# Three transformer blocks on one core: norms, values, state decays and gates of the second block's mixers at other places in the engines' orders

## The reference, cut to what matters

```python
qkv = jax.nn.silu(causal_short_conv(jnp.concatenate([a_q, a_k, a_v], -1), gdn_conv)).astype(f32)
aq = l2_normalize(to_chunks(aq, GDN_HEADS)) * (GDN_DK ** -0.5)
ak = l2_normalize(to_chunks(ak, GDN_HEADS))
o_a = from_chunks(gated_delta_rule(aq, ak, av, beta, scalar_to_chunks(g_a)))
...
o_b = from_chunks(diag_decay_linear_attention(bq, bk, bv, to_chunks(log_alpha, GLA_HEADS)))
...
o_c = from_chunks(diag_decay_linear_attention(cq, to_chunks(k_c, HGRN_HEADS), ...))
...
y = (jax.nn.sigmoid(m_a) * (o_a @ w_br_a) + jax.nn.sigmoid(m_b) * (o_b @ w_br_b)
     + jax.nn.sigmoid(m_c) * (o_c @ w_br_c))
return y @ w_out
```

## Time and profile before

| | |
|---|---|
| median of 3 runs | 4140.33 us |
| the profiled execution | 4149.57 us, of it span 4147.8 |
| TensorE busy in the span | 3614.0 us (87%) |
| VectorE, ScalarE, GpSimd busy | 1619.3, 1226.5, 170.5 us |
| mean granted clock of TensorE | 0.893 |
| the mixers of the second block | 1904.3 to 2775.2 us |
| the branches' start | 2775.2 to 2807 us |

### The profile page before, as it was taken

One profiled execution on the slowest core, in us unless ns is written; L12 is line 12 of the kernel. 1 busy time (PEld: TensorE's weight loads), 2 busy tenths in 40 slices (PEclk: granted clock), 3 DMA queues, 4 the chain that ended last, 5 costly groups with the idle time before them and its releaser, 6 DMA issues. The chain is left out here.

```text
span 4147.8 us, 67008 instructions
## 1 busy us (share of the span) xinstructions
PE 3614.0 (87%) x29006; PEld 2801.7 (68%) x29006; DVE 1619.3 (39%) x2889; ACT 1226.5 (30%) x2001; POOL 170.5 (4%) x129
## 2 busy tenths in 40 slices
PE   7888989888889989996877777769899999888998
PEld 6676767666669989994655556657678777445444
DVE  2443344434344353424434344546543343322121
ACT  2322232232222122223333445541222221233330
POOL 0000000000002010000101001120000000000000
PEclk9898889889769989997888889989899999978887
DMA  3000001000013323320111111123133333201110
GB/s 121 23 30 24 25 28 30 24 25 27 20 63 92 108 62 92 92 87 26 54 49 41 41 43 60 52 104 94 49 91 92 92 92 92 76 11 36 41 36 36
DMA packets 63590, 236.23 MB, mean 57 GB/s; under 512 B 7232, under 2 KB 7232, under 8 KB 62144
## 3 DMA queue, kind: packets, MB, share of 16 engines
q1 hardware_dynamic: 57168, 209.16, 16.7%
q0 software_dynamic: 2672, 16.50, 1.0%
q10 hardware_dynamic: 3456, 6.29, 0.4%
HBM read 219.28 MB, written 12.65 MB: 56 GB/s over the span
## 5 line engine op out<-in xcount | busy, mean ns | idle before, releaser
L405 PE MATMUL psum<-arena,ring 128*128 128x264 f32 (+2 forms) x5304 | 1625.0, 393 | 7.3 <-DVE arena L350 6.2
L405 PE MATMUL psum<-arena,arena 128*128 128x264 f32 (+1 forms) x6288 | 1538.5, 348 | 100.3 <-DVE ring L341 34.5
L405 PE MATMUL psum<-arena 32*32 32x32 f32 (+16 forms) x16392 | 1126.4, 248 | 364.3 <-ACT arena L326 112.5
L405 PEld LDWEIGHTS psum<-arena 32*32 32x32 f32 (+10 forms) x16392 | 790.4, 138 | 714.1 <-issue 317.2
L405 PEld LDWEIGHTS psum<-arena,arena 128*128 128x128 f32 x6288 | 1040.4, 194 | 277.8 <-issue 83.2
L405 PEld LDWEIGHTS psum<-arena,ring 128*128 128x128 f32 (+1 forms) x5304 | 966.3, 196 | 255.9 <-issue 127.3
L334 ACT ACTIVATE arena<-psum 128x512 f32<-128x512 f32 (+12 forms) x601 | 268.0, 446 | 1046.4 <-PE psum L405 905.1
L341 DVE TENSOR_TENSOR ring<-ring,arena 128x1024 fp32r<-128x1024 f32 (+1 forms) x301 | 362.3, 1204 | 475.3 <-ACT arena L334 470.7
L341 DVE TENSOR_TENSOR arena<-arena 128x528 f32<-128x528 f32 (+9 forms) x692 | 330.9, 478 | 411.0 <-ACT arena L326 262.1
L334 ACT ACTIVATE arena<-ring 128x1024 fp32r<-128x1024 f32 (+1 forms) x301 | 308.8, 1026 | 569.0 <-PE psum L405 513.7
L341 DVE TENSOR_TENSOR arena<-arena,psum 88x192 f32<-88x192 f32 (+4 forms) x428 | 193.4, 452 | 573.9 <-PE psum L405 566.0
(11 more groups left out here) (35 smaller groups left out, 680.1 us busy)
## 6 DMA issues: line engine op xcount, KB each, us to landing
ring<-in_w SPq DMA_DIRECT2D x368, 512.0 KB, 3.5
bg<-arena ACTq DMA_DIRECT2D x24, 256.0 KB, 2.0
ring<-in_w SPq DMA_DIRECT2D x24, 256.0 KB, 2.6
arena<-in_x SPq DMA_DIRECT2D x2, 2112.0 KB, 11.7
arena<-bg POOLq DMA_DIRECT2D x1, 3072.0 KB, 16.8
od<-arena POOLq DMA_DIRECT2D x8, 264.0 KB, 2.3
arena<-od POOLq DMA_DIRECT2D x1, 2112.0 KB, 8.8
out<-arena SPq DMA_DIRECT2D x1, 2048.0 KB, 6.3
```

The costliest lines, as they stand in the source:

```text
L405: self.last_ins = self.eng.matmul(out, l, r, start=start, stop=stop, skip_group_check=skip)
```

## The change

Six things:

1. `delta()`: the sum of squares of q is issued after k's projection, that of k after v's; ScalarE's and VectorE's parts are placed accordingly, with the copies and subtractions for the next weights ahead of silu and convolution.
2. `delta()`: `gd_kk`, `gd_kq` and the transposes of v and k come before `gd_row` and wait for the scaled keys (`gd_qk`) alone; the decay matrices are made behind them, the exp `gd_er` last.
3. `linear()`: the gate's projection stands before the transposes of the values; the gate's silu and the copy of the transposed values are both after them.
4. `decay_attention`: `la_last`, the exps and `la_qi` are part of the last level's step.
5. Gates: their banks are emptied by a copy. The sigmoids are taken in the branches, in place, one behind each slab's high copy.
6. O's split: both halves on VectorE, 11 of 12 pieces at the end of VectorE's `delta()`, one per step as they become ready, the twelfth at the start of the branches. GpSimd's 12 subtractions are gone.

The diff, cut to its core:

```diff
+    def values(off, r, i, gate):
         yield from glin(off, ("la_proj", r, "v", i), ("la_vt", r, i))
         yield
+        yield from glin(off + SLAB, ("la_proj", r, "g", i), gate)
         P.wait_ge(*at("la_vt", r, i))
         b = P.bank(1, "la_v", r, i)
...
-            for i, nme in enumerate("qkv"):
-                yield from glin(off + i * SLAB, ("gd_proj", hd, i), ("gd_pad", hd, i))
-                if hd == 0:
-                    (rates, sums, turned)[i]()
-                if nme != "v":
-                    yield
-                    P.colsum(("gd_sum", hd, i), ("gd_root", hd, i), c["ones"], [U.n0 if nme == "q" else U.u], T, [("gd_sq", hd, i)])
+            def squares(i):
+                P.colsum(("gd_sum", hd, i), ("gd_root", hd, i), c["ones"], [U.u if i else U.n0], T, [("gd_sq", hd, i)])
+
+            yield from glin(off, ("gd_proj", hd, 0), ("gd_pad", hd, 0))
+            if hd == 0:
+                rates()
+            yield
+            yield from glin(off + SLAB, ("gd_proj", hd, 1), ("gd_pad", hd, 1))
+            if hd == 0:
+                sums()
+            squares(0)
+            yield
+            yield from glin(off + 2 * SLAB, ("gd_proj", hd, 2), ("gd_pad", hd, 2))
+            if hd == 0:
+                turned()
+            squares(1)
+            yield
...
-            P.wait_ge(*at("gd_ct"))
-            b = P.bank(1, "gd_diff", hd)
-            for j in range(4):
-                P.mm(bk(b)[:, J4[j]], s16[0:16, 4 * j + hd, :], m.CT[0:16])
-            P.did("gd_row", hd)
-            yield
-
-            P.wait_ge(*at("gd_qi", hd))
+            P.wait_ge(*at("gd_qk", hd))
             four(("gd_kk", hd), ("gd_A", hd), U.k, U.k)
             four(("gd_kq", hd), ("gd_M", hd), U.k, U.q)
-            P.wait_ge(*at("gd_conv", hd, 2))
             P.wait_ge(*at("gd_silu", hd, 2))
...
+            yield
+            P.wait_ge(*at("gd_ct"))
+            b = P.bank(1, "gd_er", hd)
+            for j in range(4):
+                P.mm(bk(b)[:, J4[j]], s16[0:16, 4 * j + hd, :], m.CT[0:16])
+            P.did("gd_row", hd)
...
-            A.act(m.sg, bk("b_gate", i), ACT.Sigmoid, "b_gate", i)
+            A.copy(m.sg, bk("b_gate", i), "b_gate", i)
...
-                x = (U.q, U.k, U.v)[i]
                 A.act(x, x, ACT.Silu, "gd_silu", hd, i)
...
+                if i < 2:
+                    A.act(U.u if i else U.n0, x, ACT.Square, "gd_sq", hd, i)
+
+            def root(i):
+                A.wait_ge(*at("gd_sum", hd, i))
+                A.inv_root(U.wT if i else U.n1, bk("gd_root", hd, i), "gd_root", hd, i, bias=c["eps6"])
...
+            act_more(K, m.wx)
+            yield
+            silu(0)
...
+            act_more(K, m.wx)
+            yield
+            silu(1)
+            root(0)
...
+            act_more(K, m.wx)
+            yield
+            silu(2)
+            root(1)
...
-            A.wait_ge(*at("gd_row", hd))
-            A.act(U.er, bk("gd_diff", hd), ACT.Exp, "gd_er", hd)
+            yield
             A.wait_ge(*at("gd_diff", hd))
             A.act(U.DT, U.D, ACT.Relu, scale=-1.0)
             A.act(U.D, U.D, ACT.Relu)
-            A.act(U.D, U.D, ACT.Exp, scale=-1.0)
-            A.act(U.DT, U.DT, ACT.Exp, "gd_decay", hd, scale=-1.0)
-            yield
+            A.act(U.D, U.D, ACT.Exp, "gd_decay", hd, scale=-1.0)
+            A.act(U.DT, U.DT, ACT.Exp, "gd_decayt", hd, scale=-1.0)
+            A.act(U.er, bk("gd_er", hd), ACT.Exp, "gd_er", hd)
```

```diff
+            else:
+                cu = v4(W.cum)
+                A.wait_ge(*at("la_last", r))
+                A.act(W.E, W.E, ACT.Exp)
+                A.act(m.el[:, 0:4].unsqueeze(2), cu[:, :, 127:128], ACT.Exp)
+                A.act(W.cum, W.cum, ACT.Exp, "la_exps", r)
             yield GATES
         gate_out()
-        cu = v4(W.cum)
-        A.wait_ge(*at("la_last", r))
-        A.act(W.E, W.E, ACT.Exp)
-        A.act(m.el[:, 0:4].unsqueeze(2), cu[:, :, 127:128], ACT.Exp)
-        A.act(W.cum, W.cum, ACT.Exp, "la_exps", r)
...
+        act_more(K, m.wx)
+        yield
+        yield
         A.wait_ge(*at("la_vtr", r, i))
+        A.act(m.Gt[i], bk(*gate), ACT.Silu, *gate)
         A.copy(m.V[i], bk("la_v", r, i), "la_v", r, i)
...
+            dve_more(K, m.wx)
+            conv(0)
...
+            dve_more(K, m.wx)
+            conv(1)
...
+            V.wait_ge(*at("gd_root", hd, 0))
+            V.stt(U.q, U.q, 128.0 ** -0.5, U.n1, MUL, MUL)
+            yield
+            dve_more(K, m.wx)
...
+            V.wait_ge(*at("gd_root", hd, 1))
+            V.stt(U.k, U.k, 1.0, U.wT, MUL, MUL, "gd_qk", hd)
+            yield
...
+            V.wait_ge(*at("gd_row", hd))
+            V.tt(v4(U.D), v4(bk("gd_er", hd)), col("cu"), SUB, "gd_diff", hd)
+            V.wait_ge(*at("gd_decay", hd))
+            V.tt(v4(U.D), v4(U.D), bc4(c["slo"]), MUL)
+            for j, J in enumerate(J4):
+                V.stt(U.A[:, J], bk("gd_A", hd)[:, J], G["nbe"][:, 4 * j + hd:4 * j + hd + 1], U.D[:, J], MUL, MUL, *(("gd_A", hd) if j == 3 else ()))
+            V.wait_ge(*at("gd_decayt", hd))
+            V.tt(v4(U.DT), v4(U.DT), bc4(c["triu"]), MUL)
+            V.tt(U.M, bk("gd_M", hd), U.DT, MUL, "gd_M", hd)
+            V.wait_ge(*at("gd_er", hd))
+            V.tt(U.qi, U.q, U.er, MUL, "gd_qi", hd)
...
+            ready.add(hd)
+        for j in range(11):
+            while j not in ready:
+                yield
+            split_dve(V, m.Oh_r[j][:], m.O[:, j * T:j * T + T], m.O_r[j][:], "b_Osplit", j)
+            yield
...
+            else:
+                cu = v4(W.cum)
+                V.wait_ge(*at("la_K", r, n))
+                V.tt(v4(W.E), cu[:, :, 127:128].to_broadcast([128, 4, 128]), cu, SUB, "la_last", r)
+                V.wait_ge(*at("la_s", r, n - 1, heads - 1))
+                V.wait_ge(*at("la_exps", r))
+                V.tt(W.Kz, W.k, W.E, MUL)
+                V.tt(W.Q, W.q, W.cum, MUL, "la_qi", r)
...
-        cu = v4(W.cum)
-        V.wait_ge(*at("la_K", r, len(LV) - 1))
-        V.tt(v4(W.E), cu[:, :, 127:128].to_broadcast([128, 4, 128]), cu, SUB, "la_last", r)
-        V.wait_ge(*at("la_exps", r))
-        V.tt(W.Kz, W.k, W.E, MUL)
-        V.tt(W.Q, W.q, W.cum, MUL, "la_qi", r)
```

```diff
+GATE_PART = (0, 1, 2, 2, 3, 3, 3, 3)
...
-        pe_lin3(K, m.wb, i, ("b_y", i), m.Oh_r, m.O_r, [("b_Olow", j) for j in range(12)], 4, 4 * (i % 3))
+        pe_lin3(K, m.wb, i, ("b_y", i), m.Oh_r, m.O_r, [("b_Osplit", j) for j in range(12)], 4, 4 * (i % 3))
...
+        if i < 24:
+            A.wait_ge(*at("b_gates", GATE_PART[i // 3]))
+            g = m.bg[:, i * T:i * T + T]
+            A.act(g, g, ACT.Sigmoid, "b_sigma", i)
...
+    split_dve(V, m.Oh_r[11][:], m.O[:, 11 * T:12 * T], m.O_r[11][:], "b_Osplit", 11)
...
-            if k == 0:
-                for j in range(4 * br, 4 * br + 4):
-                    V.cp(m.Oh_r[j][:], m.O[:, j * T:j * T + T], "b_Ohi", j)
...
-            V.wait_ge(*at("b_gates", (0, 1, 2, 2, 3, 3, 3, 3)[k]))
+            V.wait_ge(*at("b_sigma", i))
...
-    for j in range(12):
-        G.wait_ge(*at("b_Ohi", j))
-        G.tt(m.O_r[j][:], m.O[:, j * T:j * T + T], m.Oh_r[j][:], SUB, "b_Olow", j)
```

95 lines of the change are left out of this document (41 added, 54 removed).

## The result

The changed kernel takes 4023.75 us, the median of 4 runs (4008.05 to 4039.47), beside 4149.93 us for the kernel before (4 runs, 4138.51 to 4168.02). The ratio is 0.9692, with a 95% interval of 0.9636 to 0.9748: 3.1% faster. The forecast was 4008, range 3968 to 4078. The profiled execution took 4039.47 us, span 4037.7: 110.1 us less than the profiled one of before. It is the slowest of the four, 15.7 us above their median; the medians differ by 126.2 us.

A forecast was written before the change was run, and what follows sets the result against it. TensorE bounds the mixers: busy 651.57 of 870.90 us, plus 219.3 standing still. 4149.6 - 100.4 (idle) + 10 (blocking) - 30 (clock) - 14.6 (branches) + 1.3 (load) = 4015.9; less 9.2 to the median, 4008 forecast, range 3968 to 4078.

The forecast's parts named there:

- Norms: Delta heads: sums of squares issued after the next projection cover TensorE's waits, 45.9 us to 6.5, -39.4 us.
- Keys: Delta heads: key products stop waiting for VectorE's products, -17.7 us; A's transposes wait for the later decay chain, +21.6.
- Values: The gate's projection ahead of the values' transposes removes their waits, 8.3 us to 0.
- State: Decay attentions: state decays moved one level up cut waits before Kz's transposes from 29.4 us to 2, -27.4.
- Gates and low halves: Mixers: emptying gate banks by copy saves ScalarE 37 table loads; bank waits -9.1 us, weights' low-half waits -24.6.
- (f): What stays or grows in the mixers: softplus blocking +7 us, level products by GpSimd -0.5, output norms -2.
- Clock: Mixers: 18 fewer waits of 2 us or more, at 2.1 us of full speed each, -38, of which -30 taken.
- Branches: Branches' start: with one split left, TensorE starts near 2781.9 and ends three slabs near 2792.3, not 2807: -14.6 us.
- Splits: Output casts and subtractions on VectorE in the mixers: 0 for those under a projection, level hold-ups within +10 us.
- rival 1: Mixers: half comes back, as every move hands a wait to the next instruction; 4071 us, chance 0.20.
- (e): Gates emptied by copy in the mixers: -9.1 us for bank waits, -24.6 for the weights' low halves.
- the slower one: ScalarE's weights' high copies get behind the norms' roots; 26 more such waits use up the gain, 34 give 4181; chance 0.03.

The follow-up runs named there:

- u2: The changed kernel with each sum of squares again right behind its own projection on all three engines: 4104.14 us, mixers 60.8 us longer.
- a2: The kernel before with only the norms changed (each sum of squares behind the next projection): 4088.03 us, mixers 819.9 us.
- u3: The changed kernel with the row and decay matrices again ahead of the key products: 4036.07 us, mixers 10.1 us longer.
- u4: The changed kernel with the values' transposes again ahead of the gate's projection: 4036.47 us, mixers 762.6 us.
- u5: The changed kernel with the last difference, exps and products for the state again behind the last level: 4060.68 us, mixers 32.9 us longer.
- a1: The kernel before with only the gates changed (banks emptied by a copy, sigmoids in the branches): 4126.23 us, mixers 852.8 us.
- u1: The changed kernel with the gates' sigmoids back in the mixers: 4077.46 us, mixers 42.9 us longer.
- n2: The changed kernel with the last part of the gates' transfer (3 MB) issued only after the branches' fourth slab: 4018.6 us, slabs 4 to 12 in 25.0 us.
- u6: The changed kernel with O's split again at the branches' start, casts on VectorE, subtractions on GpSimd: 4027.72 us, mixers 10.3 us shorter.

## Why the prediction was right, point by point

The direction and the largest terms (norms, state decays, the branches' start) held. The values and the keys did not, and the low halves came back for another reason than the one given.

- **Norms** (-39.4): by shape 58.2 to 24.5, but this holds two things. The squares' own waits went from 45.9 to 2.0, and the first head's 9.90 us stands elsewhere, 11.9 together, where I left 6.5. u2 and a2 show that the part is worth more than its waits: the low halves went with it, which I had credited to the gates.
- **Keys** (-17.7 and +21.6): A's transposes wait 19.4 us, the size of the estimate. But the sum of the two, a loss of 4, had the wrong sign: u3 shows a gain of 10, since in the new order of the rest the key products would wait 32.5 us and not 19.2. Of the key products' waits one is left, 8.55 us in the fourth head, behind the softplus; I had left 1.5.
- **Values** (-8.3): the wait went, of the gain the traces show 0 to 4 us (u4; its other executions leave it open). This step failed: I took the 6.19 us behind a softplus for a wait of the transposes. I read one of the output norms' 7.87 us in the trace after as the same chain.
- **State** (-27.4): 29.4 to 1.8 us, as forecast; u5 confirms it.
- **Gates and low halves** (-9.1 and -24.6): 49.7 to 20.2 us, forecast 16. The number came out, its cause did not: the low halves went with the norms' order (a2 21.2 us, u2) and hardly with the table loads (a1 4.3, u1 0.7). What the gates gave instead lies mostly in the decay levels (20.5 of 35.0 us of idle time in u1), for which (f) has -0.5. That the two errors nearly cancel in the sum is luck.
- **Softplus** (+7) and output norms (-2): the norms went up, from 12.3 to 22.5, with two waits of 7.9 where there were 0.0 and 0.9, since the softplus now ends there; some of the others fell. The waits that stand behind a softplus were 8.9, 7.1 and 6.2 before and are 7.9, 7.9, 7.0 and 8.6 now, +9.2 with the values' among them: the mechanism was right and the size near.
- **Idle time** 219.3 to 133.7, forecast 119 and 10 for blocking that no row showed: 129. **Clock** -22.6 for -30. Of the waits of 2 us and more 19 are left, where I expected 24 (of 41 by the instructions, 42 by my count), so each one gone gave about 1.0 us and not the 2.1 of the earlier trace rows: this term was mis-sized twice, and the errors cancel in part. The mixers come out at 762.6 for 750.5.
- **Branches**: -16.1 for -14.6 up to the third slab. TensorE starts 4.6 us behind the mixers, not 6.7 as in the forecast (2781.9, for which the terms shown give no sum), and needs 11.1 us and not 10.4 for the three slabs. The +4.6 behind it was missed: I had asked only whether the gates would be late, not whether their transfer would make the weights late once three slabs ran ahead in half the time (n2).
- **Splits**: I counted nothing for those under a projection; u6 shows about 6 us in the last round. I had left what they hold up in the levels to the +10.
- **Table load before ln1** (+1.3): it is in the order and in nothing that a total shows.
- The sum of the steps was 4015.9 against the profiled execution's 4039.5; of the 23.6 us, 12.1 are in the mixers, 4.6 in slabs 4 to 12, 8.4 (9.7 less the 1.3 counted) in the code ahead of the mixers and behind slab 12, which holds no edit but the load and the sigmoids of slabs 13 to 24 (33.3 us before, 33.7 after), and -1.5 is the start.
- **From the sum to the median**: I took 9.2 off because the profiled execution lay above the median of three runs. With four runs that median is 4149.93, with the seven or eight beside the experiments 4149.4 to 4150.5, so the execution was an ordinary one and the term is void; it widened the miss. From median to median the change gave 126.2 us, where the parts add up to 133.7, 7.5 us more. That this is closer than the 23.6 above is the spread of the executions, of which the traced one was the slowest.
- **Signs**: met were 54 table loads, Kz under 5, a wait before A's transposes in all four heads (4.25 three times, 6.65), clock above 0.88 and the branches' first wait; missed were idle time of 110 to 130 (133.7) and column sums under 15 us (24.5). The sum of the waits for masked copies and GpSimd did not grow (25.7 to 24.4). One sign of being wrong came: nine slabs of the branches took 29.5 us, 3.3 each and not 2.77 (n2).

The time lies a quarter of the way from the forecast to rival 1 (half comes back). Rival 1's own sum is short: low halves that gain nothing cost the 24.6 of (e) and not 17, so it stood for 4079, just outside the range. Of the others, the slower one (high copies behind the roots) did not show: six waits for low halves, not 26 more. TensorE's busy time fell by 22.6 us; by the rule of the Trainium skill (TensorE: Matmul & The Clock Gate, "Terms") I had worked out -52, so the trace does not bear it out here. Nor does it with the clocks as measured: 0.86 over 870.90 us and 0.89 over 762.60 give 122 and 84 us by the same rule of the Trainium skill, an estimate of -38. The clock records of the two traces say why: TensorE stood still for 69 of the 240 us at half clock before and for 37 of the 165 after, so half of the remainder, 86 and 64 us, was lost, 22 less. And the drain that the Trainium skill has behind a table load (ScalarE: Activation LUTs, "What ACT_TABLE_LOAD costs") is missing in this trace too: the load at 2501.05 in the fourth head took 1.28 us, and the activation behind it starts at 2502.34.

```profile
2501.05 1.28 ACT L322 ACT_TABLE_LOAD   x1
...
2502.34 1.39 ACT L326 ACTIVATE arena<-arena 128x512 f32<-128x512 f32 x2
```
